# FFN in-projections with the token tile stationary and 512 weight columns moving, the gated product transposed on TensorE

## The reference, cut to what matters

```python
x = x + 0.5 * swiglu_ffn(rms_norm(x, g1), w_in1, w_out1)
x = x + mixer(rms_norm(x, g2))          # layer 0: pooling and convolution; layer 1: spatial gating
x = x + 0.5 * swiglu_ffn(rms_norm(x, g3), w_in2, w_out2)

def swiglu_ffn(x, w_in, w_out):         # w_in 1024 x 5632 (gate | up), w_out 2816 x 1024
    gate, up = split(x @ w_in, 2)
    return (silu(gate) * up) @ w_out
```

## Time and profile before

| | us |
|---|---|
| median of 3 runs | 940.22 (940.21 to 940.26) |
| span of the profiled execution, first to last instruction | 938.5 |
| TensorE busy | 927.6 |
| VectorE busy | 522.7 |
| ScalarE busy | 411.9 |
| bytes moved by DMA | 170.36 MB, 182 GB/s in the mean |

### The profile page before, as it was taken

One profiled execution on the slowest core, in us unless ns is written; L12 is line 12 of the kernel. 1 busy time (PEld: TensorE's weight loads), 2 busy tenths in 40 slices (PEclk: granted clock), 3 DMA queues, 4 the chain that ended last, 5 costly groups with the idle time before them and its releaser, 6 DMA issues.

```text
span 938.5 us, 15299 instructions
## 1 busy us (share of the span) xinstructions
PE 927.6 (99%) x6505; PEld 872.2 (93%) x6505; DVE 522.7 (56%) x464; ACT 411.9 (44%) x413; POOL 26.7 (3%) x44
## 2 busy tenths in 40 slices
PE   8999999999999999999999999999999999999997
PEld 7999999989989999999999999999999899999995
DVE  5765545446967665455547444554478475454533
ACT  6453334326744544333435344334364265343322
POOL 1500000000000000000000000000010000000000
PEclk9999999999999999999999999999999999999999
DMA  8985555523512875676518656556184277556501
GB/s 264 310 270 179 179 179 201 196 75 120 172 46 101 303 241 180 217 236 202 179 45 278 217 179 213 184 197 190 46 288 161 90 242 263 185 177 209 196 7 45
DMA packets 124213, 170.36 MB, mean 182 GB/s; under 512 B 2773, under 2 KB 108777, under 8 KB 124168
## 3 DMA queue, kind: packets, MB, share of 16 engines
q1 hardware_dynamic: 124168, 169.69, 54.1%
HBM read 168.63 MB, written 1.05 MB: 181 GB/s over the span
## 4 chain that ended last, share of the span: by engine, by line
PE 96%; issue 1%; DVE 1%; DMA 1%; ACT 1%; POOL 0%; SPq 0%; POOLq 0%; ACTq 0%; DVEq 0%
PE ub L894 10%; PE ub L896 10%; PE ub L895 10%; PE ga L894 10%; PE ga L896 10%; PE ga L895 10%; PE acc L894 10%; PE acc L895 10%; PE acc L896 10%; PE ga L1093 1%; PE tp L955 1%; DMA raw<-in_ffn_w_in_dram 1%; PE ub L1093 1%; PE tp L1180 0%; DVE w_lo L607 0%
## 5 line engine op out<-in xcount | busy, mean ns | idle before, releaser
L607 DVE TENSOR_TENSOR w_lo<-raw,w_hi 128x2048 fp32r<-128x2048 f32 (+1 forms) x154 | 352.1, 2295 | 246.3 <-ACT w_hi L410 246.1
L410 ACT ACTIVATE w_hi<-raw 128x2048 fp32r<-128x2048 f32 (+1 forms) x154 | 292.1, 1902 | 91.9 <-PE acc L896 61.5
L894 PE MATMUL ub<-xn_hi,w_hi 128*128 128x256 f32 x688 | 195.1, 284 | 0.0
L894 PE MATMUL ga<-xn_hi,w_hi 128*128 128x256 f32 x688 | 194.8, 283 | 0.2 <-ACT sgh L455 0.2
L896 PE MATMUL ub<-xn_hi,w_lo 128*128 128x256 f32 x688 | 194.7, 283 | 0.0
L895 PE MATMUL ub<-xn_lo,w_hi 128*128 128x256 f32 x688 | 194.7, 283 | 0.0
L896 PE MATMUL ga<-xn_hi,w_lo 128*128 128x256 f32 x688 | 194.7, 283 | 0.0
L895 PE MATMUL ga<-xn_lo,w_hi 128*128 128x256 f32 x688 | 194.7, 283 | 0.0
L894 PE MATMUL acc<-w_hi,act_hi 128*128 128x512 f32 x416 | 163.6, 393 | 0.0
L895 PE MATMUL acc<-w_lo,act_hi 128*128 128x512 f32 x416 | 162.3, 390 | 0.0
L896 PE MATMUL acc<-w_hi,act_lo 128*128 128x512 f32 x416 | 161.9, 389 | 0.0
(11 more groups left out here) (130 smaller groups left out, 766.0 us busy)
## 6 DMA issues: line engine op xcount, KB each, us to landing
raw<-in_ffn_w_in_dram SPq DMA_DIRECT2D x88, 1024.0 KB, 5.1
raw<-in_ffn_w_out_dram SPq DMA_DIRECT2D x44, 1024.0 KB, 5.0
raw<-in_sgu_w_in_dram SPq DMA_DIRECT2D x8, 1024.0 KB, 5.3
raw<-in_ab_w_in_dram SPq DMA_DIRECT2D x6, 1024.0 KB, 4.9
raw<-in_ab_w_out_dram SPq DMA_DIRECT2D x4, 1024.0 KB, 4.8
raw<-in_sgu_w_out_dram SPq DMA_DIRECT2D x4, 1024.0 KB, 7.1
gain<-in_ffn_norm_dram SPq DMA_DIRECT2D x4, 512.0 KB, 5.8
xres<-in_x_dram SPq DMA_DIRECT2D x2, 512.0 KB, 6.3
```

Of the source, the lines that this page charges most:

```text
L410: act.activation(w_hi[:, n % RING, o:], raw[:, n % RAW, o:], ACT.Copy).then_inc(hi_split, 1)
L607: dve.tensor_tensor(w_lo[:, n % RING, o:], raw[:, n % RAW, o:], w_hi[:, n % RING, o:].bitcast(F32), ALU.subtract).then_inc(lo_split, 1)
L894: pe.matmul(dst, s_hi, m_hi, start=start, stop=False)
```

## The change

The in-projections of the FFNs, the first four slabs of mix1 and the slabs 0, 1, 4 and 5 of mix0 now have the token tile stationary and 512 weight columns moving. A slab of such a pair holds half of K (4 blocks of 128 rows) for 512 columns: 256 of gate and 256 of up. Token tile 0 goes to bank `ga` and tile 1 to `ub`, each a whole bank (`row[t]`).

`unit` does one pair: tile 0 through both slabs, then, once the earlier product is complete, the four transposes of the step before (`turned`, into bank `tp`), then tile 1 through both slabs. ScalarE gates each tile by itself (`gate_rows`, 256 columns) and VectorE multiplies each (`product_rows`), which now frees `ga` and `ub`. High and low parts are made from the transposed product in PSUM (`hidden_hi`, `hidden_lo`). Each slab is loaded by two DMAs of 512 KB.

```diff
-                sp.dma_start(raw[:, n % RAW, :].rearrange("p (c n) -> p c n", n=src.shape[-1]), src)\
-                    .then_inc(raw_landed[n % RAW], 16)
+                for a in range(2):
+                    sp.dma_start(dst(raw[:, n % RAW, :])[a], src[a]).then_inc(raw_landed[n % RAW], 16)
...
             # ScalarE, an FFN
                 split_to(b + 3)
-                    gate(b, f, ACT.Silu)
+                    gate_rows(0, b, r, f, ACT.Silu)
                     split_to(b + 5)
-                    (high part of the turned product)
+                    gate_rows(1, b, r, f, ACT.Silu)
                     split_to(b + 7)
                     with act.Fori(0, (STEPS - 3) // 2) as i:
                         for j in range(2):
-                            gate(n, f + s, ACT.Silu, i)
+                            gate_rows(0, n, r + s, f + s, ACT.Silu, i)
+                            hidden_hi(j, j, e + j, i)
                             split(n + 6, i)
-                            product_hi(s % 2, f + s, i)
+                            gate_rows(1, n, r + s, f + s, ACT.Silu, i)
                             split(n + 7, i)
                             split(n + 8, i)
...
             # VectorE, an FFN
-                    split_to(b + 4)
-                    product(b + 1, f, e)
+                    product_rows(0, g, e)
                     split_to(b + 5)
-                    (low part of the turned product)
+                    product_rows(1, g)
                     split_to(b + 7)
                     with dve.Fori(0, (STEPS - 3) // 2) as i:
                         for j in range(2):
+                            product_rows(0, g + 2 * s, e + s, i)
+                            hidden_lo(j, j, e + j, i)
                             split(n + 6, i)
-                            product(n + 1, f + s, e + s, i)
-                            product_lo(s % 2, e + s, i)
+                            product_rows(1, g + 2 * s, e + s, i)
                             split(n + 7, i)
                             split(n + 8, i)
...
             # TensorE
+            def rows_in(n, t, half, fresh=None, between=None):
+                tok = slice(t * P, (t + 1) * P)
+                for a in range(4):
+                    c, o = 4 * half + a, slice(a * WIDE, (a + 1) * WIDE)
+                    mm = three(row[t], xn_hi[:, c, tok], xn_lo[:, c, tok], w_hi[:, n % RING, o],
                                w_lo[:, n % RING, o], c == 0, c == KD - 1)
...
+            def unit(n, f, i=None, between=None):
+                slab_ready(n, i)
+                pe.wait_ge(ga_free, at(f, 2, i))
+                rows_in(n, 0, 0)
+                slab_ready(n + 1, i)
+                rows_in(n + 1, 0, 1).then_inc(first_rows, 1)
+                pe.wait_ge(ub_free, at(f, 2, i))
+                if between is not None:
+                    between()
+                rows_in(n, 1, 0).then_inc(slab_used, 1)
+                rows_in(n + 1, 1, 1).then_inc(slab_used, 1)
...
+                    def step(j, start, i=None):
+                        n = b + 2 + 3 * j
+                        unit(n, f + 1 + j, i, lambda: turned(tp[j]))
+                        step_out(n + 2, j, e + 1 + j, start, i)
```

More of the change, by code:

```diff
@@ L21 @@
 WIDTH = 256
+WIDE = 512
 RAW = 3
@@ L57, in hybrid_trunk @@
     banks_of = {"ffn": STEPS, "mix0": 4, "mix1": 4}
-    base, fill0, ffn0 = [0], [0], [0]
+    units_of = {"ffn": STEPS, "mix0": 2, "mix1": 2}
+    gated_of = {"ffn": 2 * STEPS, "mix0": 2, "mix1": 0}
+    base, fill0, ffn0, unit0, gated0 = [0], [0], [0], [0], [0]
     for kind, *_ in stages:
@@ L68, in hybrid_trunk @@
         order += [("norm", k, t, h) for t in range(TT) for h in range(2)]
-        if kind != "mix1":
+        if kind == "mix0":
             order += [("hidden", k)]
@@ L262, in turn @@
                             n, s = b + 2 + 3 * j, 1 + j
-                            load(n, wi[:, :, bass.ds(i * (2 * WIDTH) + s * WIDTH, WIDTH)], run)
-                            load(n + 1, wi[:, :, bass.ds(i * (2 * WIDTH) + (FF + s * WIDTH), WIDTH)], run)
-                            load(n + 2, wo[:, bass.ds(i * 4 + 2 * (s - 1), 2), :], run)
+                            for a in range(2):
+                                load_rows(n + a, w_in, a, pair(s * WIDTH, FF, i), run)
+                            load_out(n + 2, w_out, bass.ds(i * 4 + 2 * (s - 1), 2), run)
                     turn(0, None)
@@ L515, in _ @@
                     split_to(b + 6)
[L517 to L521, removed]
+                    for t in range(TT):
+                        if t == 0:
+                            act.wait_ge(first_rows, r + 2)
+                        else:
+                            act.wait_ge(slab_used, b + 6)
+                        act.activation(u[:, t, :], row[t], ACT.Copy).then_inc((ga_free, ub_free)[t], 1)
+                        split_to(b + 7 + t)
                     act.activation(warm[:, :], ident[:, 0:1], ACT.Silu)
@@ L567, in _ @@
                 else:
[L568 to L571, removed]
-                        act.activation(xs[:, :, j * WIDTH:(j + 1) * WIDTH], bank[:, :, :], ACT.Gelu)\
-                            .then_inc(free, 1)
-                        split_to(b + (4, 7, 8, 9)[j])
+                    for j in range(2):
+                        for t in range(TT):
+                            if t == 0:
+                                act.wait_ge(first_rows, r + j + 1)
+                            else:
+                                act.wait_ge(slab_used, b + 2 * j + 2)
+                            act.wait_ge(small_full, small[("norm", k, 1, 1)] + 1)
+                            act.activation(xs[:, t, j * WIDE:(j + 1) * WIDE], row[t], ACT.Gelu)\
+                                .then_inc((ga_free, ub_free)[t], 1)
+                            split_to(b + (4, 7, 8, 9)[2 * j + t])
                     act.wait_ge(mix1_landed, 16 * 3)
@@ L787, in _ @@
                         tap(1)
-                    product(b + 3, f + 1, out=conv_in[:, 2:4, LEAD:])
+                    product(b + 3, f + 1, conv_in[:, 2:4, LEAD:])
                     split_to(b + 5)
@@ L981, in hidden, with turned @@
+            def turned(bank):
+                for j in range(2):
+                    for t in range(TT):
+                        o = j * T + t * P
+                        mm = pe.transpose(bank[:, o:o + P], sgh[:, 1, t, j * P:(j + 1) * P], ident[:, :])
+                mm.then_inc(hidden_full, 1)
             def hidden(k, f):
@@ L999, in full_in, with tail @@
                 slab_in(n, open_bank(n, which, f, i, per)).then_inc(slab_used, 1)
-            def tail(k, slabs, ready, start=None):
+            def tail(k, slabs, ready, start=None, late=None):
                 for t in range(TT):
@@ L1006, in tail @@
                         last = a == len(slabs) - 1
+                        if t == 0 and a == 1 and late is not None:
+                            late()
                         if t == 0:
@@ L1152, in _ @@
                 else:
-                    first_pair(k, f)
-                    for j in range(2, 4):
-                        bank, free = ((ga, ga_free), (ub, ub_free))[j % 2]
-                        slab_ready(b + j)
-                        pe.wait_ge(free, f + 1)
-                        for t in range(TT):
-                            mm = slab_in_rows(b + j, bank, t)
-                        mm.then_inc(slab_used, 1)
+                    first_unit(k, f)
+                    unit(b + 2, f + 1)
                     full_in(b + 4, 0, f + 2)
```

248 lines of the change are left out of this document (139 added, 109 removed).

## The result

The changed kernel took 943.1 us in the median of 4 runs (941.8 to 946.78), the kernel before 940.22 (940.14 to 940.26). The ratio is 1.0038, with an interval of 1.0026 to 1.005: slower by 0.4%, and by more than the 0.2% that can be told. The forecast was 941.4, with a range of 935.5 to 947.5, and "slower" was given the largest chance (0.42). The profiled execution of after is the fastest of the four, 941.8 with a span of 940.1. The working of the prediction stands beside that one. The 1.3 us up to the median are a matter of their own: runs of before lie within 0.3 us of each other, runs of after 5 us apart.

What follows compares the result with a forecast made beforehand. The prediction took the time as the sum of TensorE's own instructions. A matmul gain of 12.8 us, net of the added transposes, against some 14 us of new waits gave +1.2: 941.4 us, range 935.5 to 947.5.

Steps and rivals of the forecast that it cites:

- The pace of 512 columns: In-projection matmuls: 4608 of 256 columns become 2304 of 512, each saving 0.0132 us, a gain of 30.4 us.
- The groups: Transposes of the product in the FFNs: 40 more groups of four at 0.44 us each, a cost of 17.6 us.
- rival D: Something costs time in all 40 steps, transpose groups at 0.60 us or small waits: 946 to 949 us, chance 0.10.
- The steady step: FFN steps behind the opening: no waits, period 16.77 us instead of 16.98; four FFNs together give -5.4 us.
- Stage 2's opening: Opening of the FFN after mix0: ends 28.15 us after its first matmul, against 24.35 before, so +3.8 us.
- Stages 3 and 5: Openings of the FFN after an FFN and the one after mix1: ends at 24.9 and 27.6, +0.55 and +3.0 us.
- Stage 0: Opening of the first FFN: slab 7's low part comes at 40.35 us, against 38.76 before, so +1.6 us.
- All waits: TensorE's new waits in the four FFN openings, for two products and a low part: some 14 us in total.
- Mixers: mix0 and mix1: -1.0 us, with a wait of 0.25 in it, and -1.28 us, together -2.3 us.
- rival C: Slab halves land later, +1.1 us per landing, six landings in the FFN openings, 6.6 us: 948 us, chance 0.13.
- rival E: TensorE's granted clock falls for 2 us in three places after new mid-kernel waits: +3 us, chance 0.05.
- rival B: Landings are short, slab 7 always in 5.1 us, so the FFN openings end sooner: 935.7 us, chance 0.22.

Runs made afterwards that it cites:

- e6_narrow: e2_order with each 512-column in-projection matmul of the pairs done as two of 256 columns (2304 more): 956.73 us.
- e5_turn2: e2_order with every group of four transposes of the product done twice (44 groups more): 947.19 us.
- e2_order: The changed kernel with ScalarE's and VectorE's lists in order of need in the FFN openings, and one split of mix0 moved: 928.38 us, ratio 0.9877.
- e4_halves: The kernel before with each slab loaded by two DMAs of 512 KB, nothing else changed: 940.08 us, ratio 1.0001.
- e9_filled2: e3_gates with 12 TensorE matmuls on constants ahead of the first out slab of each FFN: 947.36 us, ratio 1.0075.
- e1_again: The changed kernel run again without any edit, for the spread of its time: 944.14 us, ratio 1.0052.
- e10_filled_after: The changed kernel with TensorE matmuls on constants in the places of its opening waits: 945.16 us, ratio 1.0053.
- e3_gates: The changed kernel with only the two bank-freeing products moved early, the turned product's low part still behind slabs 6 and 7: 951.97 us, ratio 1.0121.

## Why the prediction was right, and where only by luck

The mechanism was right, and so was its place: the profiled execution came out at 941.8 with 941.4 forecast. By its steps, with openings against the 24.1 to 24.5 and 38.60 that the trace of before really has (the prediction took 24.36, 24.35 and 38.76, from model or chain, which was up to 0.24 too long):

- **The pace of 512 columns**: 0.2267, as taken; saved per pair 0.0123 instead of 0.0132 (e6_narrow), so 28.4 us, not 30.4. The rule that the prediction took from the Trainium skill ("TensorE: Matmul & The Clock Gate", section "Back-to-back issue gap"), by which the time would have been 966, is the page's gap of a matmul by itself; these matmuls, each with a new stationary tile, don't keep it: the rows decided rightly.
- **The groups**: 0.43 to 0.44 each (e5_turn2). Nothing recurs in a steady step, so rival D is out.
- **The steady step**: 16.80, not 16.77. The rest of an FFN gave -1.0 and not -1.35 (the -5.4 over four; the 0.0132 unrounded would have given -1.31). Four stages: 1.4 us less gained than forecast.
- **Stage 2's opening**: ended at T + 27.84; forecast T + 28.15. Slab 7 was issued at T + 15.15 (15.2) and split 5.33 before the end (5.25); its landing took 7.4 and not 7.7. The wait for `ga` was 1.3 (1.2), for the transposes 2.0 (3.2, since slab 5 took 5.7 and not 6.7), and the last 1.0 (0.55).
- **Stages 3 and 5**: ended at T + 24.14 and 26.99; forecast 24.9 and 27.6. Both issues of slab 7 came when forecast (12.95 and 15.72, for 13.0 and 15.7); it landed in 5.9 each time where 6.7 and 6.6 had been taken. That is the whole difference.
- **Stage 0**: 39.55, forecast 40.35. Slab 7 was issued at 28.96 instead of 29.8; its landing took 5.3 (5.1). Some 0.2 of this is the very first slab, in at 9.6 here and at 9.9 in before.
- **All waits**: the ten come to 10.4 us, and with 0.2 for each that the list leaves out (below) to 12.4, which is what the openings have above e2_order's; forecast were some 14.
- **Mixers**: -1.6, forecast -2.3. In mix0 the wait costs more than the 0.25: mix0 takes 87.28, and 86.64 in e2_order, where the product stands behind the split, so 0.64. The list of waits shows 0.2 of it, for it counts idle time only, and the matmul ahead of a wait is listed at 0.39 us where its share of a dense row is 0.23. In stages 2, 3 and 5 the openings exceed e2_order's by 4.8, 1.15 and 4.0 us with 4.2, 1.0 and 3.4 us of waits in them: some 0.2 us for each wait on top of what is listed.
- **Halves, rival C**: no cost (e4_halves), as taken.
- **The clock, rival E**: it did not fall in the profiled execution of after, as forecast. But the reasoning was weak, and here luck had a part. The rows of before show an idle time in which no work followed: still 1.00 until 3.8 us after it began. They can't show a fall that comes behind a shorter one, when TensorE works again. In e9_filled2 it fell behind 2.2 us of idling, 3.0 us after it had begun; in e1_again 2.1 left the profiled execution at 1.00. And the longest wait was 2.0, not 3.2. In the slowest executions of after and e1_again the mean clock is 0.995, so it did fall there: rival E, with its 0.05 and +3, took part in these.

The openings cost 1.8 less than taken (7.2 for 8.95), steady steps and mixers gave 2.1 less, and the two cancelled: a figure met within 0.4 us, from terms off by up to 1.4. Against the median it is off by 1.7.

Two sizes in the rivals don't come out of the prediction's own times. B ends stage 0 at 39.7 with slab 7 in 5.1, but the forecast has 5.1 there too and ends at 40.35; so B is 936.4, not 935.7. C counts stage 2 twice, though there only slab 7's landing ends last (the out slab would come at 28.7 by slab 5, at 29.25 by slab 7); so it is 5.5 us and not 6.6. And one sign of being wrong, a landing of slab 7 under 5.5, was met in stage 0 (5.3), where the forecast itself has 5.1: it contradicts the forecast that it was to guard.

One thing was not forecast at all: the spread of the runs. A kernel whose openings end with a landing inherits the landing's scatter, and it is one-sided for a profile that happens to be the fastest of four. The 1.3 us from 941.8 to the median of 943.1 are this spread, at an equal clock (0.999 in three of the four), and they carried the result past the 0.2%. The landings of the profiled execution were short in stages 3 and 5 (5.9 and 5.9 us), towards rival B; in e1_again they were 6.3 and 6.9, in e10_filled_after 7.4 and 6.9.

The change itself is worth 12 us. It lost them to an order of two lists that suited the old first consumers: before the change nothing small was needed before slab 4, with it three small operations are.

## What to carry to other kernels

When a change makes an engine need new small operations, place them in the other engines' lists by the time at which they are needed, ahead of the splits or loads that are needed later; count what stands ahead of each, and what that waits for. What is put behind them is later too, and with it the load that it sets free: in e3_gates this took 1.6 us, in e2_order nothing that was needed. Take away all waits of an opening together, beginning with the last: with one left, the others' time collects in it, and a single long idle of TensorE costs more than several short ones, since the granted clock can fall behind it. The median of a kernel that waits on a landing needs more runs, and its profiled execution may be the lucky one.

## What the runs showed of the hardware

- After 4.33 us of idling TensorE in e3_gates ran at half clock for about 3.4 us (0.50 in 324 to 326, 1.00 again from 328); such a fall cost 1.5 to 2.3 us in each of four openings. Around the ten waits of up to 2.0 us in after's profiled execution the windows show 1.00 throughout, after 2.2 us of idling in e9_filled2 they show a fall, 0.8 us after TensorE took up work again, so which waits bring it on is not settled by their length alone. The Trainium skill ("TensorE: Matmul & The Clock Gate", "Part 1: The HAM clock gate") has 1.2 GHz as the clock of an idle TensorE, and says that the number of matmuls at the lower clock at a kernel's start differs from run to run. That the clock of one kernel differs from run to run the six runs of e10_filled_after show as well (0.995 to 0.999).
- Matmuls on constants in the idle time keep the clock up without making the opening longer, where they are shorter than the wait (e9_filled2: in three stages, with up to 1.75 us left, the clock stayed up; in the fourth 2.2 us were left, and it fell).
- A matmul of 128 columns on the float32 constants stands as two instructions (24 of them as x48), each 0.11 us from start to start: from 509.45 to the next matmul at 514.73. A transpose of the same size stands as one, of 0.11 us (x4, 0.44).
- Loads as two DMAs of 512 KB in flight cost the kernel before nothing (ratio 1.0001), and each landed in 4.4 to 4.5 us in the median, where one of 1 MB took 5.1.
